# Adding x1 in the store's place: four y buffers, an accumulating DMA, and VectorE turning hid in the final stage of an expert-choice MoE layer

## The chip, the cores and the metric

The kernel runs on one core of a Trainium2 chip. The metric is the device time of one execution in microseconds. The core has TensorE (PE: matmuls and, in its own row, weight loads), VectorE (DVE), ScalarE (ACT), GpSimd (POOL) and SyncE (SP). SP and POOL issue the DMAs; the DMAs of both run on 16 DMA engines.

## What is computed

One encoder layer for two groups of 1024 tokens with 1024 columns, all in float32. A first part (token mixer) leaves `x1`, the residual stream, and `h2`, its normed and modulated form, in DRAM. The part that matters here is the last line of the layer:

```
x = x + gate2 * rmsnorm(expert_choice_moe(h), g_post_ffn)

def expert_choice_moe(h, w_router, w_gate, w_up, w_down):
    aff = jax.nn.softmax((xf @ w_router), axis=-1)
    gate, idx = lax.top_k(aff.T, cap)              # 16 experts, 128 rows each per group
    xe = xf[idx]
    hid = silu(xe @ w_gate) * (xe @ w_up)          # per expert
    ye = (hid @ w_down) * gate[..., None]
    y = zeros.at[idx].add(ye)                      # scatter-add into y
```

Each group picks its own 128 rows for every expert. A row of `y` is final when the last expert that picked it has been added. The result row is `x1 + rows * y / sqrt(mean(y*y) + eps)`, where `rows` is gate2 times the gain.

## The kernel before, in words

The stage `experts` (names with `moe_`) goes through experts 0 to 15 in order, both groups at a time. Experts 0 to 7 run in a loop on every engine, 8 to 15 are written out. Every float32 product is made of three products of a high and a low part, so each 1024x1024 weight matrix (GATE, UP, DOWN) comes as four pieces of 1 MB (`wf`), is rounded by ACT (`w_hi`, function `split`) and subtracted by DVE (`w_lo`, function `split`). A piece takes 24 matmuls of PE (PIECE 2 x 3 products x 4 banks). The PE order per expert e is UP(e), GATE(e+1), DOWN(e): 288 matmuls of 128x512.

Before DOWN(e), `hid` (128 rows by 1024 columns for each group) must be turned so that its columns lie on partitions. There are two ways in the kernel:

- Experts 0 to 7: DVE turns it with 16 transposes (`turn_h`, line 2581) into `h_raw`, ACT copies `h_hi` from it (`h_out`, line 2423), DVE subtracts `h_lo` (line 2587). PE starts DOWN with `down_first`, which waits for `h_hi_ready`.
- Experts 8 to 15 (`is_late`, LATE = 8): PE turns it with 16 transposes of 128x128 against the identity (`turn_h`, line 2754) into the PSUM banks, between the second and third piece of GATE(e+1); ACT and DVE take it out of PSUM (`turned_out`, lines 2411 and 2559).

From expert 9 on, final rows are put out beside the experts' work: the "window" of expert e holds four units, the last two experts' windows end at unit 25. A unit is 128 rows: units 0 to 15 are plain blocks of 128 tokens (valid for what experts up to 8 have added), units 16 to 25 are the row lists of experts 9 to 14, written again over the earlier rows; units 26 and 27 (expert 15's rows) come after the last matmul. For each unit, in the kernel before:

- POOL loads y into `fy` and x1 into `fx` (`load_unit`, lines 2337 to 2342), two buffers each; unit n waits for the store of unit n-2.
- ACT squares and sums `fy` (`square`, line 2458), DVE makes the mean (`mean`, line 2602), POOL takes the power -0.5 (`root`, line 2352).
- DVE scales (line 2610) and adds x1 (line 2616), both in `result`; POOL stores (`store_unit`, lines 2359 and 2365). The stores of one group's row lists wait for each other, since a row may stand in two lists.

POOL runs everything in written order: it waits for the scatter-add of expert e-1, loads two units, gathers half of expert e+2's rows, takes two roots, stores two units, the same again for the other two, and then issues the two scatter-adds of expert e (`scatter`, line 2325). ACT has its squares between pieces of weights, DVE its means and results. In the body of expert 15, POOL loads the last two units of the window (24 and 25), then y and x1 of units 26 and 27 (`load_last`), and only then takes roots and stores.

## Time and profile before

| what | value |
|---|---|
| device time, median of 3 runs | 2362.34 us (2360.07 to 2362.45) |
| device time of the profiled execution | 2362.63 us |
| its span, first to last instruction | 2360.9 us |
| PE busy | 2255.7 us (96%) |
| DVE busy | 1349.1 us (57%) |
| ACT busy | 1100.5 us (47%) |
| POOL busy | 730.6 us (31%) |
| mean granted TensorE clock | 0.988 of full speed |

The span is what the trace covers; the device time is 1.73 us more. Busy time is the sum of an engine's instructions; in the timeline a row's bracket is the idle time before it and who ended it. DMA-issuing instructions of POOL appear with the time that making their descriptors took. "To landing" is the time from a DMA's issue to its completion.

### The profile page before, as it was taken

The page shows a single profiled execution, that of the slowest core. Times are in us where ns is not written, and L with a number is a line of the kernel's source. Part 1 is how long each engine was busy: PE and PEld are TensorE (multiplying, and loading weights), DVE is VectorE, ACT ScalarE, POOL GpSimd, SP SyncE. Part 2 cuts the span into 40 slices and gives each one's busy share as a digit, 9 for nine tenths or more (in the row PEclk, how much of TensorE's full clock was granted, in tenths as well). Part 3 has the DMA queues.
Part 4 walks back from the last instruction along what each step waited for, and adds up shares of the span by engine and source line. Part 5 has one row for each costly group of instructions (what it writes and reads, how often), then busy time and mean ns, then how long its engine had stood idle before and what let it go on. Part 6 is the DMA issues. An engine that isn't in the chain of part 4 may idle for free. (4 is left out here: it accounts for less than half of the span.)

```text
span 2360.9 us, 34620 instructions
## 1 busy us (share of the span) xinstructions
PE 2255.7 (96%) x13219; PEld 1876.9 (79%) x13219; DVE 1349.1 (57%) x1995; ACT 1100.5 (47%) x1782; POOL 730.6 (31%) x770
## 2 busy tenths in 40 slices
PE   6999999999999999999984999999999999999997
PEld 4679989867899898677763888888888888888885
DVE  3212344555422436665557877777777667677665
ACT  4212434555534436665542544544444455545552
POOL 3004241434233515340003222221222333443634
PEclk9999999999999999999996999999999999999998
DMA  8745445657554459764538666766667678988785
GB/s 314 265 114 184 153 148 192 188 137 185 139 188 152 148 172 247 225 183 162 169 128 313 215 218 231 248 223 224 209 224 244 229 267 316 334 311 302 286 304 178
DMA packets 224095, 511.49 MB, mean 217 GB/s; under 512 B 38420, under 2 KB 129444, under 8 KB 204496
## 3 DMA queue, kind: packets, MB, share of 16 engines
q1 hardware_dynamic: 174576, 394.78, 49.3%
q0 software_dynamic: 49376, 114.78, 16.5%
q8 instruction: 92, 1.51, 0.3%
q14 instruction: 51, 0.42, 0.1%
HBM read 415.32 MB, written 93.69 MB: 216 GB/s over the span
## 5 line engine op out<-in xcount | busy, mean ns | idle before, releaser
L2553 DVE TENSOR_TENSOR moe_w_lo<-moe_wf,moe_w_hi 128x2048 fp32r<-128x2048 f32 x192 | 437.2, 2288 | 252.4 <-ACT moe_w_hi L2404 251.5
L2404 ACT ACTIVATE moe_w_hi<-moe_wf 128x2048 fp32r<-128x2048 f32 x192 | 366.0, 1915 | 436.7 <-PE moe_acc L2734 424.1
L2734 PE MATMUL moe_acc<-moe_w_hi,moe_x_hi 128*128 128x512 f32 x1024 | 400.1, 391 | 2.9 <-DVE moe_w_lo L2553 2.0
L2734 PE MATMUL moe_acc<-moe_w_lo,moe_x_hi 128*128 128x512 f32 x1024 | 399.2, 390 | 0.0
L2734 PE MATMUL moe_acc<-moe_w_hi,moe_x_lo 128*128 128x512 f32 x1024 | 399.1, 390 | 0.0
L2734 PEld LDWEIGHTS moe_acc<-moe_w_hi,moe_x_hi 128*128 128x128 f32 x1024 | 192.6, 188 | 43.7 <-DVE moe_w_lo L2553 2.4
L2734 PEld LDWEIGHTS moe_acc<-moe_w_hi,moe_x_lo 128*128 128x128 f32 x1024 | 192.6, 188 | 40.1
L2734 PEld LDWEIGHTS moe_acc<-moe_w_lo,moe_x_hi 128*128 128x128 f32 x1024 | 192.5, 188 | 39.7
L1793 PE MATMUL banks<-fr_w_hi,fr_h_hi 128*128 128x256 f32 x768 | 223.2, 291 | 0.0
L1793 PE MATMUL banks<-fr_w_lo,fr_h_hi 128*128 128x256 f32 x768 | 217.0, 283 | 0.0
L1793 PE MATMUL banks<-fr_w_hi,fr_h_lo 128*128 128x256 f32 x768 | 216.9, 282 | 0.0
L2308 POOL DMA_INDIRECT moe_xe<-scratch_h,moe_parts x120 | 181.5, 1513 | 86.8 <-issue 77.3
L1784 PE MATMUL banks<-fr_h_hi,fr_w_hi 128*128 128x512 f32 x496 | 204.3, 412 | 1.9 <-DVE fr_h_lo L1381 1.1
L1784 PE MATMUL banks<-fr_h_hi,fr_w_lo 128*128 128x512 f32 x496 | 194.2, 392 | 0.0
L1784 PE MATMUL banks<-fr_h_lo,fr_w_hi 128*128 128x512 f32 x496 | 193.7, 391 | 0.0
L1030 ACT ACTIVATE fr_stage<-banks 128x512 f32<-128x512 f32 (+1 forms) x114 | 67.4, 591 | 270.9 <-PE banks L1784 145.8
L1362 DVE TENSOR_TENSOR fr_w_lo<-fr_w_raw,fr_w_hi 128x1024 fp32r<-128x1024 f32 x56 | 71.2, 1274 | 209.3 <-ACT fr_w_hi L1018 209.3
L906 POOL DMA_DIRECT2D fr_v<-scratch_vov x224 | 156.2, 746 | 81.9 <-PE banks L1963 80.5
L2734 PE MATMUL moe_acc<-moe_w_hi,moe_h_hi 128*128 128x512 f32 x448 | 174.4, 389 | 0.0
L2734 PE MATMUL moe_acc<-moe_w_hi,moe_h_lo 128*128 128x512 f32 x448 | 174.3, 389 | 0.0
L2734 PE MATMUL moe_acc<-moe_w_lo,moe_h_hi 128*128 128x512 f32 x448 | 174.3, 389 | 0.0
L1793 PEld LDWEIGHTS banks<-fr_w_hi,fr_h_hi 128*128 128x128 f32 x768 | 146.8, 191 | 4.9 <-issue 4.8
(312 smaller groups left out, 4306.7 us busy)
## 6 DMA issues: line engine op xcount, KB each, us to landing
moe_wf<-in_w_expert_gate SPq DMA_DIRECT2D x64, 1024.0 KB, 5.3
moe_wf<-in_w_expert_up SPq DMA_DIRECT2D x64, 1024.0 KB, 6.0
moe_wf<-in_w_expert_down SPq DMA_DIRECT2D x64, 1024.0 KB, 6.8
fr_w_raw<-in_w_units SPq DMA_DIRECT2D x28, 1024.0 KB, 6.7
fr_bias<-in_na_bias SPq DMA_DIRECT2D x16, 1520.0 KB, 11.7
fr_a_w<-in_w_ada POOLq DMA_DIRECT2D x16, 1024.0 KB, 8.4
scratch_qk_t<-fr_stage SPq DMA_DIRECT2D x64, 256.0 KB, 2.5
scratch_vov<-fr_stage SPq DMA_DIRECT2D x96, 128.0 KB, 2.4
```

The source lines that it names most:

```text
L906: pool.dma_start(v[j][p0:CHUNK, CH_AT[rb] + n, :], v_view[2, m, r0:r0 + k, cols_, :]).then_inc(nv_loaded[j], 16)
L1030: nc.scalar.activation(out, product, ACT.Copy).then_inc(evac_done, 1)
L1362: nc.vector.tensor_tensor(w_lo[:, h % 2, k, :], w_raw[:, h % 2, k, :], w_hi[:, h % 2, k, :].bitcast(F32), ALU.subtract).then_inc(w_lo_read ...
L1784: mm = nc.tensor.matmul(ps[:, b % 2, :], w[x1][:, slot, k, a * P:(a + 1) * P], h[x2][:, k, t * HALF:(t + 1) * HALF], start=start, stop=stop)
L1793: mm = nc.tensor.matmul(ps[:, b % 2, part * QW:(part + 1) * QW], h[x1][:, k, tile:tile + P], w[x2][:, slot, k, :], start=(k == 0 and i == ...
L2308: pool.indirect_dma_start(quarter_rows(g)[:, t, :], None, h2_quarters, bass.IndirectOffsetOnAxis(ap=at, axis=0)).then_inc(gathered[g], 16)
L2404: nc.scalar.activation(w_hi[:, q, :, :], wf[:, q, :, :], ACT.Copy).then_inc(w_hi_ready, 1)
L2553: nc.vector.tensor_tensor(w_lo[:, q, :, :], wf[:, q, :, :], w_hi[:, q, :, :].bitcast(F32), ALU.subtract).then_inc(w_lo_ready, 1)
L2734: mm = nc.tensor.matmul(acc[:, j, b, :], x[:, g, k, :], w[:, q, a, h * HALF:(h + 1) * HALF], start=(k == 0 and i == 0), stop=(k == KC - 1 ...
```

## The change

It does four things.

- `fx` is gone and `fy` has four buffers (SLOTS = 4). `load_unit` loads y alone; unit n waits for the store of unit n-4. A window's four loads are issued together, then the whole gather, four roots, four `add_x1`, four stores.
- x1 is added to the scaled `fy` in SBUF by a DMA that accumulates (`add_x1`, new), issued by POOL when DVE has scaled the unit; the store waits for that DMA. DVE's add (line 2616) stays only for unit 26.
- The mean of units 0 to 25 is made by POOL in `root` (a multiply-add before the power) and no longer by DVE.
- `hid` of experts 8 to 14 is turned by DVE as it is for 0 to 7; only expert 15's is still turned by PE. ACT's squares move behind DOWN pieces 1 and 2, DVE's scalings behind DOWN pieces 2 and 3.

```
-    LATE = 8
+    SLOTS = 4
...
-        fy = s.sb("fy", [P, 2, D])
-        fx = s.sb("fx", [P, 2, D])
+        fy = s.sb("fy", [P, SLOTS, D])
...
-            return (fy[:, n % 2, :], fx[:, n % 2, :]) if n < LAST else (xe[:, n - LAST, :], ye[:, n - LAST, :])
+            return (fy[:, n % SLOTS, :], fy[:, n % SLOTS, :]) if n < LAST else (xe[:, n - LAST, :], ye[:, n - LAST, :])
...
             def load_unit(n):
-                j = n % 2
                 g, t, e = units[n]
-                if n >= 2:
-                    pool.wait_ge(out_stored[j], 16 * (n // 2))
+                if n >= SLOTS:
+                    pool.wait_ge(*used(out_stored, n - SLOTS))
+                loaded = used(fy_loaded, n)[0]
                 if t is not None:
-                    pool.dma_start(fy[:, j, :], y_view[t]).then_inc(fy_loaded[j], 16)
-                    pool.dma_start(fx[:, j, :], x1_view[t]).then_inc(fx_loaded[j], 16)
+                    pool.dma_start(fy[:, n % SLOTS, :], y_view[t]).then_inc(loaded, 16)
                 else:
                     at = bass.IndirectOffsetOnAxis(ap=index_c[:, col(e, g)], axis=0)
-                    pool.indirect_dma_start(fy[:, j, :], None, io["y"], at).then_inc(fy_loaded[j], 16)
-                    pool.indirect_dma_start(fx[:, j, :], None, io["x1"], at).then_inc(fx_loaded[j], 16)
+                    pool.indirect_dma_start(fy[:, n % SLOTS, :], None, io["y"], at).then_inc(loaded, 16)
+
+            def add_x1(n):
+                g, t, e = units[n]
+                pool.wait_ge(y_scaled, n + 1)
+                added_x1 = used(x1_added, n)[0]
+                if t is not None:
+                    pool.dma_start(fy[:, n % SLOTS, :], x1_view[t], accum_op=ALU.add).then_inc(added_x1, 16)
+                else:
+                    at = bass.IndirectOffsetOnAxis(ap=index_c[:, col(e, g)], axis=0)
+                    pool.indirect_dma_start(fy[:, n % SLOTS, :], None, io["x1"], at, compute_op=ALU.add).then_inc(added_x1, 16)
 
...
             def root(n):
-                pool.wait_ge(y_mean, n + 1)
-                nc.gpsimd.tensor_tensor(y_r[:, n % 2:n % 2 + 1], y_ss[:, n % 2:n % 2 + 1], mhalf[:, :], ALU.pow).then_inc(y_root, 1)
+                mean = y_ss[:, n % SLOTS:n % SLOTS + 1]
+                if n < LAST:
+                    pool.wait_ge(y_sq, n + 1)
+                    nc.gpsimd.tensor_scalar(mean, mean, 1.0 / D, EPS, ALU.mult, ALU.add)
+                    pool.drain()
+                else:
+                    pool.wait_ge(y_mean, n - LAST + 1)
+                nc.gpsimd.tensor_tensor(y_r[:, n % SLOTS:n % SLOTS + 1], mean, mhalf[:, :], ALU.pow).then_inc(y_root, 1)
 
             def store_unit(n):
-                j = n % 2
                 g, t, e = units[n]
-                pool.wait_ge(out_ready, n + 1)
+                stored = used(out_stored, n)[0]
+                if n < LAST:
+                    pool.wait_ge(*used(x1_added, n))
+                else:
+                    pool.wait_ge(out_ready, n - LAST + 1)
                 if t is not None:
-                    pool.dma_start(out_view[t], result_of(n)[1]).then_inc(out_stored[j], 16)
+                    pool.dma_start(out_view[t], result_of(n)[1]).then_inc(stored, 16)
                 else:
-                    pool.wait_ge(out_stored[j], 16 * (n // 2))
-                    if units[n - 1][0] == g:
-                        pool.wait_ge(out_stored[1 - j], 16 * ((n + 1) // 2))
+                    for m in range(n - SLOTS, n):
+                        if units[m][0] == g or m == n - SLOTS:
+                            pool.wait_ge(*used(out_stored, m))
                     at = bass.IndirectOffsetOnAxis(ap=index_c[:, col(e, g)], axis=0)
-                    pool.indirect_dma_start(io["out"], at, result_of(n)[1], None).then_inc(out_stored[j], 16)
+                    pool.indirect_dma_start(io["out"], at, result_of(n)[1], None).then_inc(stored, 16)
...
-                    for h, half in enumerate((ns[0:2], ns[2:4])):
-                        for n in half:
-                            load_unit(n)
-                        if not is_last(e, 2):
-                            gather(e + 2, j, range(h, h + 1))
-                        if is_last(e) and half:
-                            pool.wait_ge(x_turned, ONE + e * GROUPS)
-                            for g in range(GROUPS):
-                                load_last(g)
-                        for n in half:
-                            root(n)
-                        for n in half:
-                            store_unit(n)
+                    for n in ns:
+                        load_unit(n)
+                    if not is_last(e, 2):
+                        gather(e + 2, j)
+                    if is_last(e):
+                        pool.wait_ge(x_turned, ONE + e * GROUPS)
+                        for g in range(GROUPS):
+                            load_last(g)
+                    for n in ns:
+                        root(n)
+                    for n in ns:
+                        add_x1(n)
+                    for n in ns:
+                        store_unit(n)
...
                     split(e, DOWN, range(0, 1))
-                    if not is_late(e):
-                        h_out(e)
+                    h_out(e)
+                    split(e, DOWN, range(1, 2))
                     for n in ns[0:2]:
                         square(n)
-                    split(e, DOWN, range(1, 2))
-                    if is_late(e):
-                        turned_out(e - LATE, (h_hi, j), late_h_turned, late_h_hi_ready)
-                    split(e, DOWN, range(2, NP))
-
-                    silu(e + 1, 1 - j)
-                    split(e + 1, UP, range(0, 2))
+                    split(e, DOWN, range(2, 3))
                     for n in ns[2:4]:
                         square(n)
-                    split(e + 1, UP, range(2, NP))
+                    split(e, DOWN, range(3, NP))
+
+                    silu(e + 1, 1 - j)
+                    split(e + 1, UP)
...
+                j = n % SLOTS
                 dve.wait_ge(y_sq, n + 1)
-                nc.vector.tensor_scalar(y_ss[:, n % 2:n % 2 + 1], y_ss[:, n % 2:n % 2 + 1], 1.0 / D, EPS, ALU.mult, ALU.add).then_inc(y_mean, 1)
-
-            def result(n):
-                j = n % 2
+                nc.vector.tensor_scalar(y_ss[:, j:j + 1], y_ss[:, j:j + 1], 1.0 / D, EPS, ALU.mult, ALU.add).then_inc(y_mean, 1)
+
+            def scale(n):
+                j = n % SLOTS
                 dve.wait_ge(y_root, n + 1)
                 if n == 0:
                     dve.wait_ge(rows_loaded, 16 * GROUPS)
-                y_rows, x_rows = result_of(n)
-                nc.vector.scalar_tensor_tensor(y_rows, y_rows, y_r[:, j:j + 1], rows[:, units[n][0], :], ALU.mult, ALU.mult)
-                dve.drain()
+                y_rows = result_of(n)[0]
+                return nc.vector.scalar_tensor_tensor(y_rows, y_rows, y_r[:, j:j + 1], rows[:, units[n][0], :], ALU.mult, ALU.mult)
+
+            def result(n):
                 if n < LAST:
-                    dve.wait_ge(fx_loaded[j], 16 * (n // 2 + 1))
+                    scale(n).then_inc(y_scaled, 1)
                 else:
+                    scale(n)
+                    dve.drain()
                     dve.wait_ge(last_loaded[1][n - LAST], 16)
-                nc.vector.tensor_tensor(x_rows, x_rows, y_rows, ALU.add).then_inc(out_ready, 1)
+                    y_rows, x_rows = result_of(n)
+                    nc.vector.tensor_tensor(x_rows, x_rows, y_rows, ALU.add).then_inc(out_ready, 1)
...
-                    if is_late(e):
-                        split(e + 1, GATE, range(2, NP))
-                        multiply(e, j)
-                    else:
-                        split(e + 1, GATE, range(2, 3))
-                        multiply(e, j)
-                        split(e + 1, GATE, range(3, NP))
-                        turn_h(e)
+                    split(e + 1, GATE, range(2, 3))
+                    multiply(e, j)
+                    split(e + 1, GATE, range(3, NP))
+                    turn_h(e)
                     split(e, DOWN, range(0, 1))
-                    if not is_late(e):
-                        h_out(e)
-                    for n in ns[0:2]:
-                        mean(n)
-                    split(e, DOWN, range(1, 2))
-                    if is_late(e):
-                        turned_out(e - LATE, h_hi, h_lo, j, late_h_hi_ready, late_h_ready)
+                    h_out(e)
+                    split(e, DOWN, range(1, 3))
                     for n in ns[0:2]:
                         result(n)
-                    split(e, DOWN, range(2, NP))
-                    split(e + 1, UP, range(0, 2))
-                    for n in ns[2:4]:
-                        mean(n)
+                    split(e, DOWN, range(3, NP))
                     for n in ns[2:4]:
                         result(n)
-                    split(e + 1, UP, range(2, NP))
+                    split(e + 1, UP)
...
-            weighted, j = fy[:, 0, :], (LAST + 1) % 2
+            j = (LAST + 1) % SLOTS
+            weighted = fy[:, j, :]
+            dve.wait_ge(*used(out_stored, LAST + 1 - SLOTS))
...
-                    products(e + 1, GATE, 1 - j, x_hi[:, 1 - j], x_lo[:, 1 - j], first)
-                    if is_late(e):
-                        turn_h(e, j)
-                    products(e + 1, GATE, 1 - j, x_hi[:, 1 - j], x_lo[:, 1 - j], second)
-                    if is_late(e):
-                        pe.wait_ge(late_h_ready, ONE + (e - LATE) * BK + BK)
-                        products(e, DOWN, j, h_hi, h_lo)
-                    else:
-                        down_first(e, j)
-                        products(e, DOWN, j, h_hi, h_lo, range(1, NP))
+                    products(e + 1, GATE, 1 - j, x_hi[:, 1 - j], x_lo[:, 1 - j])
+                    down_first(e, j)
+                    products(e, DOWN, j, h_hi, h_lo, range(1, NP))```

What stands in VectorE's row in the window of expert 13, from the product with UP on, before (`moe_w_lo` is a piece of weights, `moe_hid` the product silu times up, `moe_h_lo` the low part of the turned hid):

```order
L2598 TENSOR_TENSOR moe_hid<-moe_hid,moe_acc 128x512 x4
L2553 TENSOR_TENSOR moe_w_lo<-moe_wf,moe_w_hi 128x2048
L2602 TENSOR_SCALAR moe_parts<-moe_parts 128x1 x2
L2553 TENSOR_TENSOR moe_w_lo<-moe_wf,moe_w_hi 128x2048
L2559 TENSOR_TENSOR moe_h_lo<-moe_acc,moe_h_hi 128x512 x4
L2610 SCALAR_TENSOR_TENSOR moe_fy<-moe_fy,moe_parts,moe_rows 128x1024
L2616 TENSOR_TENSOR moe_fx<-moe_fx,moe_fy 128x1024
L2610 SCALAR_TENSOR_TENSOR moe_fy<-moe_fy,moe_parts,moe_rows 128x1024
L2616 TENSOR_TENSOR moe_fx<-moe_fx,moe_fy 128x1024
L2553 TENSOR_TENSOR moe_w_lo<-moe_wf,moe_w_hi 128x2048 x4
```

And at the same place in the changed kernel (line 2566 is the piece of weights, 2594 the transposes, 2600 the low part, 2624 the scaling):

```order
L2611 TENSOR_TENSOR moe_hid<-moe_hid,moe_acc 128x512 x4
L2566 TENSOR_TENSOR moe_w_lo<-moe_wf,moe_w_hi 128x2048
L2594 STREAM_TRANSPOSE moe_h_raw<-moe_hid 32x16x32 x16
L2566 TENSOR_TENSOR moe_w_lo<-moe_wf,moe_w_hi 128x2048
L2600 TENSOR_TENSOR moe_h_lo<-moe_h_raw,moe_h_hi 128x1024 x2
L2566 TENSOR_TENSOR moe_w_lo<-moe_wf,moe_w_hi 128x2048 x2
L2624 SCALAR_TENSOR_TENSOR moe_fy<-moe_fy,moe_parts,moe_rows 128x1024 x2
L2566 TENSOR_TENSOR moe_w_lo<-moe_wf,moe_w_hi 128x2048
L2624 SCALAR_TENSOR_TENSOR moe_fy<-moe_fy,moe_parts,moe_rows 128x1024 x2
L2566 TENSOR_TENSOR moe_w_lo<-moe_wf,moe_w_hi 128x2048 x4
```

Sixteen transposes came in ahead of DOWN's first piece, the means and the adds of x1 are gone, the first two scalings stand one piece of DOWN later, and the other two now come before UP's pieces.

What POOL issues at the program's end before, from the loads of units 24 and 25 on (`moe_xe` and `moe_ye` here are y and x1 of units 26 and 27):

```order
L2341 DMA moe_fy<-scratch_y,moe_parts 128x1024
L2342 DMA moe_fx<-scratch_x,moe_parts 128x1024
L2341 DMA moe_fy<-scratch_y,moe_parts 128x1024
L2342 DMA moe_fx<-scratch_x,moe_parts 128x1024
L2347 DMA moe_xe<-scratch_y,moe_parts 128x1024
L2348 DMA moe_ye<-scratch_x,moe_parts 128x1024
L2347 DMA moe_xe<-scratch_y,moe_parts 128x1024
L2348 DMA moe_ye<-scratch_x,moe_parts 128x1024
L2352 TENSOR_TENSOR moe_parts<-moe_parts 128x1 x2
L2365 DMA out<-moe_fx,moe_parts 2048x1024 x2
L2352 TENSOR_TENSOR moe_parts<-moe_parts 128x1
L2365 DMA out<-moe_ye,moe_parts 2048x1024
```

In the changed kernel (lines 2340 y, 2355 and 2356 the last units, 2362 the mean, 2366 the root, 2350 the accumulating add of x1, 2382 the store):

```order
L2340 DMA moe_fy<-scratch_y,moe_parts 128x1024 x2
L2355 DMA moe_xe<-scratch_y,moe_parts 128x1024
L2356 DMA moe_ye<-scratch_x,moe_parts 128x1024
L2355 DMA moe_xe<-scratch_y,moe_parts 128x1024
L2356 DMA moe_ye<-scratch_x,moe_parts 128x1024
L2362 TENSOR_SCALAR moe_parts<-moe_parts 128x1
L2366 TENSOR_TENSOR moe_parts<-moe_parts 128x1
L2362 TENSOR_SCALAR moe_parts<-moe_parts 128x1
L2366 TENSOR_TENSOR moe_parts<-moe_parts 128x1
L2350 DMA moe_fy<-scratch_x,moe_parts 128x1024 x2
L2382 DMA out<-moe_fy,moe_parts 2048x1024 x2
L2366 TENSOR_TENSOR moe_parts<-moe_parts 128x1
```

Two loads of x1 left the row ahead of the roots, and two adds by DMA stand between the roots and the stores of units 24 and 25.

## Rows read from the trace of the kernel before

**Rows 1.** The page: PE's busy time, share of the span, instructions.

```profile
PE 2255.7 (96%) x13219; PEld 1876.9 (79%) x13219; DVE 1349.1 (57%) x1995; ACT 1100.5 (47%) x1782; POOL 730.6 (31%) x770
```

**Rows 2.** The chain that ended last, windows of experts 9 on: start, us, what.

```profile
1928.40 1.75 PE moe_acc L2754 x16
1930.15 65.30 PE moe_acc L2734 x288
```

**Rows 3.** Stretches: PE, PEld, DVE, ACT, POOL busy, PEclk, DMA share, GB/s.

```profile
1333.00:1858.00 525.00, 525.00 (x2317) 434.69 (x2317) 395.36 (x305) 248.58 (x193) 135.50 (x106) 1.00 0.68 228
1992.00:2059.00 67.00, 67.00 (x306) 55.68 (x305) 48.60 (x36) 35.65 (x35) 25.32 (x26) 1.00 0.88 315
```

**Rows 4.** Timeline, DVE, ACT and PE, expert 6: start, us, engine, line.

```profile
1719.94 2.48 DVE L2598 TENSOR_TENSOR moe_hid<-moe_hid,moe_acc 128x512 f32<-128x512 f32 x4 [1.14 <-PE moe_acc L2734]
1724.71 11.45 DVE L2581 STREAM_TRANSPOSE moe_h_raw<-moe_hid 32x512 f32<-32x512 f32 x16
1736.19 2.29 DVE L2553 TENSOR_TENSOR moe_w_lo<-moe_wf,moe_w_hi 128x2048 fp32r<-128x2048 f32 x1
...
1736.20 2.01 ACT L2423 ACTIVATE moe_h_hi<-moe_h_raw 128x1024 fp32r<-128x1024 f32 x2 [8.90 <-DVE moe_h_raw L2581]
...
1741.50 0.39 PE L2766 MATMUL moe_acc<-moe_w_hi,moe_h_hi 128*128 128x512 f32 x1
```

**Rows 5.** Groups by line, forms apart: xcount | busy us, mean ns | idle before.

```profile
L2616 DVE TENSOR_TENSOR moe_fx<-moe_fx,moe_fy 128x1024 f32<-128x1024 f32 x26 | 31.9, 1226 | 2.3 <-issue 0.4
L2352 POOL TENSOR_TENSOR moe_parts<-moe_parts 128x1 f32<-128x1 f32 x28 | 17.5, 632 | 55.2 <-DVE moe_parts L2602 54.1 <-DVE moe_parts L2697 1.0
```

**Rows 6.** Timeline, POOL, ACT and PE, end of expert 14's window.

```profile
2288.34 0.94 POOL L2341 DMA_INDIRECT moe_fy<-scratch_y,moe_parts  x1 [1.34 <-DMA out<-moe_fx,moe_parts]
...
2296.98 1.06 ACT L2458 ACTIVATE moe_zero<-moe_fy 128x1024 f32<-128x1024 f32 x1 [4.13 <-DMA moe_fy<-scratch_y,moe_parts]
...
2305.56 0.61 PE L2734 MATMUL moe_acc<-moe_w_hi,moe_x_hi 128*128 128x512 f32 x1 [1.98 <-DVE moe_w_lo L2553]
...
2308.95 0.52 PE L2734 MATMUL moe_acc<-moe_w_hi,moe_x_lo 128*128 128x512 f32 x1
...
2346.99 0.39 PE L2734 MATMUL moe_acc<-moe_w_hi,moe_h_lo 128*128 128x512 f32 x1
```

**Rows 7.** Timeline, POOL, the program's last 60 us.

```profile
2301.10 1.81 POOL L2365 DMA_INDIRECT out<-moe_fx,moe_parts  x1 [1.18 <-DVE moe_fx L2616]
2306.47 2.07 POOL L2365 DMA_INDIRECT out<-moe_fx,moe_parts  x1 [3.56 <-DMA out<-moe_fx,moe_parts]
2308.85 1.60 POOL L2325 DMA_INDIRECT scratch_y<-moe_ye,moe_parts  x1 [0.30 <-issue]
...
2321.17 2.40 POOL L2341 DMA_INDIRECT moe_fy<-scratch_y,moe_parts  x1 [8.83 <-DMA scratch_y<-moe_ye,moe_parts]
...
2334.97 1.11 POOL L2352 TENSOR_TENSOR moe_parts<-moe_parts 128x1 f32<-128x1 f32 x2
...
2340.96 0.97 POOL L2365 DMA_INDIRECT out<-moe_fx,moe_parts  x1 [0.67 <-DVE moe_fx L2616]
2343.73 0.57 POOL L2352 TENSOR_TENSOR moe_parts<-moe_parts 128x1 f32<-128x1 f32 x1 [1.80 <-DVE moe_parts L2602]
...
2351.50 1.01 POOL L2365 DMA_INDIRECT out<-moe_ye,moe_parts  x1 [1.67 <-DVE moe_ye L2703]
```

**Rows 8.** DMA by queue, 1767 to 1779 us (an expert's two scatter-adds beside weights).

```profile
q0 software_dynamic: 288, 1.05, 49.7%
q1 hardware_dynamic: 277, 1.59, 37.6%
...
scratch_y<-moe_ye,moe_parts POOLq DMA_INDIRECT x2, 6.5
```

**Rows 9.** DMA issues, 2193 to 2303 us: xcount, median us to landing.

```profile
out<-moe_fx,moe_parts POOLq DMA_INDIRECT x7, 4.5
...
moe_fx<-scratch_x,moe_parts POOLq DMA_INDIRECT x6, 10.1
```

45 lines of the change are left out of this document (21 added, 24 removed).

## The prediction

> **What bounds the kernel now.** I read the page first: PE is busy 2255.7 of 2360.9 us [rows 1]. In the stretch that the change touches the chain that ended last is PE without a gap: 65.30 us of 288 matmuls for each expert, and between them 1.75 us of 16 transposes of `hid` [rows 2]. So an expert from 8 on takes 67.05 us, one of those before 65.3, and one matmul steps by 65.30/288 = 0.227 us. The stretches say the same: PE fills both, DVE is busy 395.36 of 525 us where it turns `hid` itself and 48.60 of 67 where PE does [rows 3]. DMA is the engine to watch beside them: its share is 0.68 in the early stretch and 0.88 in a window with units [rows 3].
>
> There are two places where PE doesn't set the time. The first is in expert 14's window: the load of unit 23 waits for a store [rows 6], its square on ACT starts at 2296.98 after waiting 4.13 us for the data, ACT's next weights are late, and PE idles 1.98 us before 2305.56. Behind that come nine matmuls, up to the one at 2308.95, which step by (2308.95-2305.56)/8 = 0.42 us and not 0.227: TensorE ran at its lower level, and lost 9*0.2 = 1.8 us more. The second is the end. PE's last matmul ends at 2346.99+0.39 = 2347.4, and POOL was by then on a chain of its own: store of unit 23 waiting for a store (2306.47), scatter-add of expert 14 (2308.85), its landing (2321.17), eight loads, roots (2334.97), store 25 (2340.96), root of unit 26 (2343.73), last store (2351.50) [rows 7]. From that last store to the end of the span are 9.4 us, which no part of the change touches.
>
> **The change, part by part.** *Turning on DVE.* PE loses 7*16 transposes, 7*1.75 = 12.25 us, all on the chain. DVE gets 16 transposes at 11.45 us per expert, and `h_lo` from SBUF. Whether PE then waits is read from expert 6, where the same order runs [rows 4]. UP ends at about U = 1719.9, where DVE begins to multiply; the transposes end at U+16.3; the weights of DOWN's first piece are ready at 1736.19+2.29 = U+18.6, `h_hi` at 1736.20+2.01 = U+18.3; PE starts DOWN at 1741.50 = U+21.6. So there are 3.0 us of slack, and nothing in a window stands ahead of this point on DVE or ACT: squares and scalings come behind DOWN's second piece. Behind it I walk the row. DVE: `h_lo` 2.35 to U+20.9, two pieces 4.6 to U+25.5, but ACT's piece comes after two squares (1.06 and a read of 0.2 each), so U+26.9; PE wants that piece at U+32.7. Two scalings at 1.28 and a piece: U+31.8, wanted at U+38.1. Slack is 5 to 6 us throughout. VectorE's busy time is 48.6+11.45-4*1.23 [rows 5] = 55 of 65.3 us. I cost this part at 12.25 us gained.
>
> *Four buffers.* Loads of a window no longer wait for stores of the same window. The squares of units 22 and 23 come from loads issued at the window's start, so the stall before UP(15) and its slow matmuls go: 1.98+1.8 = 3.8 us. PE would then end at 2347.4-12.25-3.8 = 2331.3.
>
> *x1 by an accumulating DMA.* DVE's 26 adds (31.9 us) were hidden behind PE and are worth nothing there. In their place stand 26 DMAs that read x1 and `fy` and write `fy`. The trace has no such DMA into SBUF; the nearest row is the scatter-add, 0.5 MB each. In the 12 us with two of them, queue q0 took 49.7% for 1.05 MB, that is 5.96 us of all 16 engines or 3.0 us apiece, while q1 moved 1.59 MB of weights in 37.6%, 2.8 us per MB, 1.4 us for 0.5 MB [rows 8]. Time to landing: 6.5 us for the scatter-adds when little else runs [rows 8], 10.1 for loads of x1 in the window [rows 9]. From below an add costs what the load that it replaces cost (nothing more), from above 12 us to landing, the wait from the issue of the last scatter-add to 2321.17. I take 10 us in a window and 6.5 to 7 at the end, where the weights are all in.
>
> *Means on POOL.* One more small operation of at most the root's 0.63 us [rows 5] for each unit, and one less hand-over from DVE to POOL; at the end 1.2 us for units 24 and 25 in a row, elsewhere hidden by POOL's own waits.
>
> **The end, worked out.** U is the end of UP(14). Before, UP(15) began two half pieces (5.4 us) before the idle time, at 2298.1, so U = 2298.1-43.5-1.75 = 2252.85, and the scatter-add of 14 at 2308.85 was at U+56. After, U comes six turns earlier: 2242.35. Scalings end at U+28.2, 29.5, 33.1, 34.4; their adds land near U+39 to U+46. Units 20, 22 and 23 belong to one group, so their stores go one after the other, 4.5 us each [rows 9] with 10.8 as the worst that I take: two landings, then the issue of the third (2306.47 to 2308.85 is 2.4). That gives U+52 with quick stores and U+57 with 7 us each; I take U+55, 2297.4, or 11.5 us earlier than before.
>
> From the scatter-add to the roots before were 2334.97-2308.85 = 26.1 us with eight loads, at about 1.7 us each from 2321.17. Two fall away: 22.7, and with the means 24. Root of 25 at 2321.4. Then, in place of "scale, add, scale, add" on DVE: two scalings 2.6, issue of the adds, 6.5 to 7 us to landing, two store issues and the 2.8 us that POOL took from its store (2340.96) to the root of unit 26 (2343.73). This is about 13.2 us in place of 8.8. Root of 26 at about 2334.5, against 2343.73: 9.2 us earlier. Unit 26's mean is ready long before (PE's bank for it at 2326), so POOL's chain and not PE sets the end, and all behind that root is as before. Span 2360.9-9.2 = 2351.7; the profiled execution's time lies 1.7 us above its span: **2353.4 us**. Its own 2362.63 is 0.3 above the median 2362.34, so this is 9 us or 0.4% below. Of the 16.05 us that PE gives back, 7 are lost behind POOL.
>
> The row against the rule: an indirect DMA of 0.5 MB took 6.5 us to landing with little beside it [rows 8]. The Trainium skill, "DMA: Bandwidth & Descriptors", section "Anatomy of one DMA — SWDGE (gpsimd) path", fits 2.0 us plus bytes over 436 GB/s, which makes 3.2 us for 0.5 MB. By that page the two adds at the end would land 3.3 us sooner and the time would be 2350, an estimate. The trace doesn't bear the page out for this kind of DMA.
>
> **Rivals.** *PE sets the end after all.* If adds and stores are quick, the scatter-add of 14 goes as soon as `ye` is ready, near U+48, and POOL's root of 26 is at 2327.5, when its mean is there. Then the end is PE's: 2331.3+13.5 (2347.4 to 2360.9) = 2344.8, time 2346.5. For it speaks that the loads of units 24 and 25 took about 5 us in the quiet end; against it that three stores of one group and the adds in front of them can hardly all fit into 48-28 us. 13 in 100.
>
> *The adds are slow and eat the gain.* In expert 15's body ACT takes the squares of 24 and 25 before it takes the turned `hid` out of PSUM. By my walk unit 25 is in at 2317.5 and squared at 2318.5, and PE needs the low part at 2331.3-10.9 = 2320.4, with 1.9 us of work between: no slack. If the scatter-add of 14 comes 5 us later than I take it, both chains move by that, PE stalls and TensorE falls to its lower level again (1.8 us). Then 2358 to 2361. Stores that took 9 to 11 us in a busy window would do it. 15 in 100.
>
> *DMA becomes the bound: slower.* A window's DMA share of 0.88 is 59 us of work [rows 3]. Four adds in place of four loads bring 4*(3.0-1.4) = 6.4 us more: 65.4 in a period of 65.3. Each further us of DMA work is then a us of PE waiting for weights, with slow matmuls behind each stall. It decides when an add costs over 3.4 us of the 16 engines: at 4.5 us a window takes 71.4, which is 4.3 us more than 67.05, over five windows 22 us, less the 12 gained elsewhere: 2371. For it speaks the sum; against it that when busy the engines move more than the mean suggests, and that weights have slack: ACT waited for PE, not for data, before its pieces. 10 in 100. The rule that bears on it is in the Trainium skill, same page, section "Issuing engines are not separate DMA queues": transfers issued from several engines share the 16 DMA engines and interleave. By that rule, the trace agrees: the two queues' shares add up to 87% there.
>
> **How the numbers follow.** The forecast (gain of 6 to 12.5 us) gets 62 in 100, PE at the end 13, the slow adds 15, DMA as the bound 10. What a measurement of this kernel can tell from no change is about 0.2%, 4.7 us. Slow adds fall on both sides of it, mostly inside. So: faster 0.78, same 0.13, slower 0.09. The range runs from PE's bound, 2346, to the slow adds' end, 2361, and leaves out most of the DMA case.
>
> **What would show it.** Right: no matmul of line 2754's kind before expert 15; 65.3 us per expert in the chain; no idle time of PE before UP(15); the end's chain through POOL's add of x1 and its landing. Each step by itself: the scatter-add of 14 near 2297, the root of 26 near 2334, adds landing in 10 and 7 us. Wrong: idle time of PE that ended on `w_lo` or `h_hi` in windows 9 to 13, granted clock below 1 there, a DMA share near 1, or ACT's turned copy in expert 15 behind a late square.

## The result and the profile after

The changed kernel takes 2394.27 us, the median of 4 runs (2392.56 to 2396.8), against 2362.39 for the kernel before in 4 runs beside it: a ratio of 1.0138 with an interval of 1.0126 to 1.0150. It is 32 us slower, where 9 us faster was forecast. The profiled execution has a span of 2390.9 us, 30.0 more than before's 2360.9.

The page of the changed kernel, busy time of each engine, to be held against [rows 1]:

```profile
PE 2252.6 (94%) x13107; PEld 1871.0 (78%) x13107; DVE 1393.4 (58%) x2041; ACT 1098.3 (46%) x1768; POOL 768.6 (32%) x796
```

The 112 transposes of PE are gone, as the change says, and still PE is busy for almost as long. The stretches of the changed kernel from expert 9's window on say why (columns as in [rows 3]):

```profile
1858.00:2391.00 533.00, 485.61 (x2099) 399.25 (x2097) 379.93 (x302) 246.32 (x228) 229.29 (x192) 0.95 0.80 266
...
2130.00:2200.00 70.00, 64.87 (x278) 53.19 (x278) 51.59 (x40) 35.33 (x32) 33.56 (x30) 0.95 0.85 291
...
2285.00:2354.00 69.00, 58.85 (x255) 48.01 (x253) 32.57 (x21) 28.54 (x28) 33.73 (x25) 0.94 0.74 224
```

PE idles in the windows of experts 11 to 14, and the granted clock is 0.95 and 0.94 in the two stretches shown, where [rows 3] had 1.00: part of the matmuls behind each stall run at TensorE's lower level. The waits of the changed kernel, 1850 to 2391 us (who waited for whom: us in total, times, longest):

```profile
POOL out L2376 <- DMA moe_fy<-scratch_x: 61.6, 16, 5.6
...
DVE moe_fy L2624 <- POOL moe_parts L2366: 52.6, 26, 10.9
...
ACT moe_w_hi L2422 <- DMA moe_wf<-in_w_expert_gate: 36.4, 13, 4.3
POOL moe_parts L2366 <- issue: 32.0, 9, 7.3
...
PE moe_acc L2740 <- DVE moe_w_lo L2566: 18.2, 4, 5.4
```

Read from the bottom: PE waited 18.2 us in four windows (11 to 14) for the low part of a piece of weights. DVE was late with it because its scalings stand ahead of it and waited 52.6 us for POOL's roots. POOL's roots waited 32.0 us for nothing that the profile shows. And the stores waited 61.6 us for the added x1.

**One window.** POOL in the window of expert 12 of the changed kernel, from its last gather on:

```profile
2148.43 0.96 POOL L2308 DMA_INDIRECT moe_xe<-scratch_h,moe_parts  x1 [0.30 <-issue]
2149.47 0.18 POOL L2362 TENSOR_SCALAR moe_parts<-moe_parts 128x1 f32<-128x1 f32 x1
2154.97 0.57 POOL L2366 TENSOR_TENSOR moe_parts<-moe_parts 128x1 f32<-128x1 f32 x1 [5.31 <-issue]
...
2163.55 3.65 POOL L2347 DMA_DIRECT2D moe_fy<-scratch_x  x4
2169.60 0.57 POOL L2376 DMA_DIRECT2D out<-moe_fy  x1 [2.40 <-DMA moe_fy<-scratch_x]
2173.66 0.55 POOL L2376 DMA_DIRECT2D out<-moe_fy  x1 [3.48 <-DMA moe_fy<-scratch_x]
2178.68 0.53 POOL L2376 DMA_DIRECT2D out<-moe_fy  x1 [4.47 <-DMA moe_fy<-scratch_x]
2183.68 0.53 POOL L2376 DMA_DIRECT2D out<-moe_fy  x1 [4.47 <-DMA moe_fy<-scratch_x]
2184.52 2.89 POOL L2325 DMA_INDIRECT scratch_y<-moe_ye,moe_parts  x1 [0.31 <-issue]
```

Between the mean (0.18 us) and the root of the first unit stands `pool.drain()`, and there 5.31 us pass. What the 16 DMA engines moved meanwhile, in the changed kernel from 2137 to 2160, in slices of 0.575 us:

```profile
GB/s 385 378 356 420 385 477 413 435 413 399 371 413 385 399 385 399 328 378 378 313 370 356 292 221 107 64 36 21 14 0 0 0 0 0 0 0 0 0 0 0
```

The last gather was issued by 2149.39; nothing is moved from the 30th slice on, 2153.7; the root starts 1.3 us later, at 2154.97. The same holds at two other long ones: nothing from about 2296.3 on and the root at 2297.32 (7.28 us behind the mean), nothing from 2363.2 on and the root at 2364.46 (6.07 behind). The weights' loads had stopped by then as well, but in the third case POOL's own loads were all that ran, and in the window of expert 10 it is the other way round: POOL's queue q0 had moved its last packets by 2010.6, the root started at 2011.56 (2.96 us of idle time), and the weights' queue q1 was 91% busy from 2010.6 to 2011.5. The drain let POOL go on only when its own DMAs were done. In the next units of a window, with nothing outstanding, it is not to be seen: mean 1.29 us, root 0.55, some 2.1 for both. What DVE and then PE do with that, in the same window:

```profile
2155.57 1.29 DVE L2624 SCALAR_TENSOR_TENSOR moe_fy<-moe_fy,moe_parts,moe_rows 128x1024 f32<-128x1024 f32 x1 [10.79 <-POOL moe_parts L2366]
...
2158.85 2.28 DVE L2566 TENSOR_TENSOR moe_w_lo<-moe_wf,moe_w_hi 128x2048 fp32r<-128x2048 f32 x1
...
2161.18 0.79 PE L2740 MATMUL moe_acc<-moe_w_hi,moe_h_hi 128*128 128x512 f32 x1 [5.13 <-DVE moe_w_lo L2566]
```

DVE stood still for 10.79 us in front of a scaling, DOWN's last piece came behind it at 2161.13, and PE had idled 5.13 us. The matmul behind the wait takes 0.79 us, not 0.39.

**POOL's round.** The chain of the changed kernel no longer runs through PE in the windows but round and round through POOL. From the scatter-add of expert 11 at 2112.30 to that of 12 at 2184.52 are 72.2 us: 19.8 until it has landed and the loads of y may go (2132.09), 17.3 for four loads and eight gathers (to 2149.4), 14.1 for means, drain and roots (to 2163.55), 21.0 for the adds, their landings one after the other and the stores. Each of these waits for the one before, and PE needs only 65.3. The scatter-adds go out at 1972.96, 2043.09, 2112.30, 2184.52: one per 69 to 72 us, and none waits for expert results any more. In the trace before, those of experts 9 to 12 all did:

```profile
2100.87 1.90 POOL L2325 DMA_INDIRECT scratch_y<-moe_ye,moe_parts  x1 [3.42 <-ACT moe_ye L2446]
```

So the round had 3.4 to 3.8 us of slack in these windows of 67.05 us, and windows of 65.3 would have left about 2, an estimate. The change put four waits for added x1 and about 12 us at the roots (14.1 in place of 4*0.63) into it.

**The window of expert 13.** It is longer still. From the scatter-add of 12 at 2184.52 to that of 13 at 2269.52 are 85.0 us. Before, these were 69.9 us (2167.96 to 2237.86), and the scatter-adds of 13 and 14 had no slack even then (0.30 us of "issue" in front of each, as in [rows 7]). The units of this window are row lists. Their four adds take POOL 9.5 us to issue, where the plain blocks' took 3.65, and stores of one group wait for each other, with nothing else of POOL's between them now:

```profile
2265.70 0.95 POOL L2382 DMA_INDIRECT out<-moe_fy,moe_parts  x1 [11.96 <-DMA out<-moe_fy,moe_parts]
```

Before, the loads and roots of the window's second half stood between the two pairs of stores, and no store waited for another store there. Against before, the scatter-adds of experts 9 to 14 are late by 6.2, 9.3, 11.4, 16.6, 31.7 and 31.9 us: half of what reaches the end arises in this one window. It is as long in kernels below that undo another part: 78.3 us with the means on VectorE, 83.1 with x1 by a plain DMA, 84.9 with PE turning. How much of it is the row of four stores alone, no run shows.

**The adds.** DMA issues and queues of the changed kernel, 2163 to 2190 (the last number of an issue is the median time to landing):

```profile
q0 software_dynamic: 902, 3.31, 53.2%
q1 hardware_dynamic: 783, 5.42, 49.0%
...
moe_fy<-scratch_x POOLq DMA_DIRECT2D x4, 512.0 KB, 11.4
out<-moe_fy POOLq DMA_DIRECT2D x4, 512.0 KB, 13.3
```

In the stretch the two queues' shares add up to 102%, against 87% in [rows 8]. The Trainium skill says in "DMA: Bandwidth & Descriptors", section "Issuing engines are not separate DMA queues", that DMAs of different issuing engines run on the same 16 DMA engines and interleave. By that rule, the trace agrees. Over all 16 direct adds the median is 12.4 us to landing, with 13.2 for the stores behind them. ACT waits for GATE's weights there, the 36.4 us above; it is not what PE waited for.

**The end.** POOL, ACT, DVE and PE of the changed kernel, timeline, from the last stores of expert 14's window:

```profile
2333.82 1.12 POOL L2382 DMA_INDIRECT out<-moe_fy,moe_parts  x1 [9.97 <-DMA out<-moe_fy,moe_parts]
2339.24 1.23 POOL L2382 DMA_INDIRECT out<-moe_fy,moe_parts  x1 [4.30 <-DMA out<-moe_fy,moe_parts]
2340.78 2.55 POOL L2325 DMA_INDIRECT scratch_y<-moe_ye,moe_parts  x1 [0.30 <-issue]
...
2350.87 1.01 POOL L2340 DMA_INDIRECT moe_fy<-scratch_y,moe_parts  x1 [5.66 <-DMA scratch_y<-moe_ye,moe_parts]
...
2355.22 1.06 ACT L2474 ACTIVATE moe_zero<-moe_fy 128x1024 f32<-128x1024 f32 x1 [16.08 <-DMA moe_fy<-scratch_y,moe_parts]
...
2358.97 1.06 ACT L2429 ACTIVATE moe_h_hi<-moe_acc 128x512 fp32r<-128x512 f32 x2
2359.59 1.29 DVE L2572 TENSOR_TENSOR moe_h_lo<-moe_acc,moe_h_hi 128x512 fp32r<-128x512 f32 x2 [17.74 <-ACT moe_h_hi L2429]
...
2360.93 0.79 PE L2740 MATMUL moe_acc<-moe_w_hi,moe_h_hi 128*128 128x512 f32 x1 [13.04 <-DVE moe_h_lo L2572]
...
2374.45 0.39 PE L2740 MATMUL moe_acc<-moe_w_hi,moe_h_lo 128*128 128x512 f32 x1
```

The scatter-add of 14 is out at 2340.78, forecast 2297. The y of unit 24 stands behind it, ACT's square of unit 24 behind that, the turned `hid` of expert 15 behind the square, and PE idles 13.04 us.

**The sum.** PE's last matmul ends at 2374.84, 27.5 us later than before's 2347.38. What follows it takes 16.1 us in place of 13.5. Together 30.0. The stretch has 2099 matmuls of PE, and so has the same stretch of a kernel below in which none of them waits (the one with scatter-adds first):

```profile
1858.00:2400.00 542.00, 473.79 (x2099) 392.13 (x2097) 381.25 (x328) 246.80 (x228) 204.82 (x166) 0.98 0.79 262
```

There PE's last matmul ends at 2331.8. The 43.0 us between that and 2374.8 are 18.2+13.0 of idle time and 485.61-473.79 = 11.8 us for which matmuls took longer, the slow ones behind the waits.

### The profile page after: what moved, and what is told of

Its sections match the earlier page's. It is cut to its first block and busy times, and to the rows that moved or that the text cites. A ratio compares the mean times of both kernels' runs of the same rounds, so it can differ in the third digit from the quotient of the medians.

```text
span 2390.9 us, 34466 instructions
## 1 busy us (share of the span) xinstructions
PE 2252.6 (94%) x13107; PEld 1871.0 (78%) x13107; DVE 1393.4 (58%) x2041; ACT 1098.3 (46%) x1768; POOL 768.6 (32%) x796
## 5 line engine op out<-in xcount | busy, mean ns | idle before, releaser
L2422 ACT ACTIVATE moe_w_hi<-moe_wf 128x2048 fp32r<-128x2048 f32 x192 | 365.6, 1915 | 391.9 <-PE moe_acc L2740 330.7
L2566 DVE TENSOR_TENSOR moe_w_lo<-moe_wf,moe_w_hi 128x2048 fp32r<-128x2048 f32 x192 | 435.9, 2288 | 184.3 <-ACT moe_w_hi L2422 183.2
L2740 PE MATMUL moe_acc<-moe_w_hi,moe_x_hi 128*128 128x512 f32 x1024 | 398.7, 389 | 0.9 <-DVE moe_x_lo L2572 0.6
L2740 PE MATMUL moe_acc<-moe_w_lo,moe_x_hi 128*128 128x512 f32 x1024 | 398.4, 389 | 0.0
L2740 PE MATMUL moe_acc<-moe_w_hi,moe_x_lo 128*128 128x512 f32 x1024 | 398.4, 389 | 0.0
L2740 PEld LDWEIGHTS moe_acc<-moe_w_hi,moe_x_hi 128*128 128x128 f32 x1024 | 192.2, 188 | 41.2 <-DVE moe_x_lo L2572 0.8
L2740 PEld LDWEIGHTS moe_acc<-moe_w_hi,moe_x_lo 128*128 128x128 f32 x1024 | 192.2, 188 | 40.0
L2740 PEld LDWEIGHTS moe_acc<-moe_w_lo,moe_x_hi 128*128 128x128 f32 x1024 | 192.2, 188 | 39.9
L2308 POOL DMA_INDIRECT moe_xe<-scratch_h,moe_parts x120 | 175.9, 1466 | 86.9 <-issue 77.2
L2740 PE MATMUL moe_acc<-moe_w_hi,moe_h_hi 128*128 128x512 f32 x392 | 157.8, 403 | 31.2 <-DVE moe_w_lo L2566 18.2
L2594 DVE STREAM_TRANSPOSE moe_h_raw<-moe_hid 32x512 f32<-32x512 f32 x240 | 168.7, 703 | 4.5
L2740 PE MATMUL moe_acc<-moe_w_lo,moe_h_hi 128*128 128x512 f32 x392 | 156.3, 399 | 0.0
L2740 PE MATMUL moe_acc<-moe_w_hi,moe_h_lo 128*128 128x512 f32 x392 | 156.3, 399 | 0.0
```

The costliest lines, as they stand in the source:

```text
L2308: pool.indirect_dma_start(quarter_rows(g)[:, t, :], None, h2_quarters, bass.IndirectOffsetOnAxis(ap=at, axis=0)).then_inc(gathered[g], 16)
L2422: nc.scalar.activation(w_hi[:, q, :, :], wf[:, q, :, :], ACT.Copy).then_inc(w_hi_ready, 1)
L2566: nc.vector.tensor_tensor(w_lo[:, q, :, :], wf[:, q, :, :], w_hi[:, q, :, :].bitcast(F32), ALU.subtract).then_inc(w_lo_ready, 1)
L2594: a = nc.vector.transpose(h_raw[u * QT:(u + 1) * QT, :, :, t * QT:(t + 1) * QT], columns)
L2740: mm = nc.tensor.matmul(acc[:, j, b, :], x[:, g, k, :], w[:, q, a, h * HALF:(h + 1) * HALF], start=(k == 0 and i == 0), stop=(k == KC - 1 ...
```

## The experiments

**Which part costs it.** Four kernels undo one part each, or do one part alone. First, the changed kernel with the means of units 0 to 25 on VectorE as before:

```
             def root(n):
-                if n < LAST:
-                    pool.wait_ge(y_sq, n + 1)
-                    nc.gpsimd.tensor_scalar(mean, mean, 1.0 / D, EPS, ALU.mult, ALU.add)
-                    pool.drain()
-                else:
-                    pool.wait_ge(y_mean, n - LAST + 1)
+                pool.wait_ge(y_mean, n + 1)
...
-                    split(e, DOWN, range(1, 3))
+                    split(e, DOWN, range(1, 2))
+                    for n in ns[0:2]:
+                        mean(n)
+                    split(e, DOWN, range(2, 3))
```

> The changed kernel with one part undone: the mean of units 0 to 25 is made by VectorE again (behind DOWN's pieces 1 and 2), and GpSimd's root is one power, with no drain. Theory A (GpSimd's drain between mean and power waits for the gathers that it has just issued, 5.3 us at 2149.65, and the roots behind it are late for VectorE's scaling): PE's idle time before DOWN's last piece (5.1 us a window) goes, windows last 65.3 to 67, the time falls from 2394 to 2355 to 2372. Theory B (the accumulating DMAs alone make GpSimd's round of 71 us): the windows stay at 70 us or more and the time at 2388 to 2396.

Measured: 2369.41 us, ratio 1.0030 (1.0016 to 1.0044), 24.9 us below the changed kernel. Its waits of PE:

```profile
PE moe_acc L2742 <- DVE moe_h_lo L2567: 12.6, 1, 12.6
...
PE moe_acc L2742 <- DVE moe_w_lo L2561: 3.2, 1, 3.2
```

The stalls of the windows are down from 18.2 to 3.2 us (one, in window 14); the one in expert 15 stays. So the means on POOL carry most of the loss as the changed kernel stands, and without them it is still 0.3% slower than before.

Second, x1 brought by a plain DMA. It overwrites the scaled y, so the normed part is missing in the rows of units 0 to 25; sizes and places of all transfers stay.

```
-  pool.dma_start(fy[:, n % SLOTS, :], x1_view[t], accum_op=ALU.add).then_inc(added_x1, 16)
+  pool.dma_start(fy[:, n % SLOTS, :], x1_view[t]).then_inc(added_x1, 16)
...
-  pool.indirect_dma_start(fy[:, n % SLOTS, :], None, io["x1"], at, compute_op=ALU.add).then_inc(added_x1, 16)
+  pool.indirect_dma_start(fy[:, n % SLOTS, :], None, io["x1"], at).then_inc(added_x1, 16)
```

> The changed kernel with x1's DMA as a plain copy into fy in the place of the accumulating one: same bytes from DRAM, same waits, same order; the scaled y is overwritten, so the normed part of rows 0 to 25's units is left out of the result. Theory B: copies land in about half the time of the adds (13.7 us before), GpSimd's round gets shorter by 10 us or more, scatter-adds go out when ye is ready, windows are PE's 65.3 us, time 2345 to 2360. Theory A alone: the drain is still there, PE's stalls stay, time 2385 to 2394.

Measured: 2357.76 us, ratio 0.9988 (0.9978 to 0.9998), 36.5 below the changed kernel. The direct transfers land in 7.0 us, not 12.4, the scatter-adds of experts 9 to 12 go out every 65.3 us (1962.61, 2027.85, 2093.13, 2158.41), and PE's waits on `w_lo` are 0.5 us in all although the drain is still there. The wait in expert 15 stays with 11.0 us: the scatter-add of 14 goes at 2310.35, behind the long window 13. Either this repair or the first alone almost closes the stalls of the windows: they don't add up as prices; they are two loads on one round, for which there are 65.3 us. This undoing gives back more than the first, so neither part alone is "the" loss.

Third, the kernel before with the one line `LATE = NE - 1`, so that VectorE turns `hid` for experts 8 to 14 and nothing else changes (two buffers, x1 loaded, means on VectorE).

> The kernel before with LATE = 15 in place of 8: hid of experts 8 to 14 is turned by VectorE, everything else stays (two buffers each, x1 added and means made by VectorE). If the first part of my sum is right (12.25 us of transposes off PE, 3.0 us of slack): 65.3 us a window, PE's last matmul 12 us earlier, time 2348 to 2357. If VectorE's row is too full with its own adds and means in it: PE idle before DOWN's pieces in each window, time 2362 or more.

Measured: 2381.31 us, ratio 1.0085 (1.0068 to 1.0102): 19 us slower than before. Its waits, 1850 to 2400 us:

```profile
DVE moe_parts L2602 <- ACT moe_zero L2458: 57.5, 11, 8.4
ACT moe_zero L2458 <- DMA moe_fy<-scratch_y: 43.5, 8, 7.4
...
PE moe_acc L2734 <- DVE moe_w_lo L2553: 19.1, 7, 9.5
...
PE moe_acc L2734 <- DVE moe_x_lo L2573: 6.4, 4, 1.8
```

With two buffers the round goes through VectorE: results come 12 us later behind the transposes, so the stores, the next loads, ACT's squares and the means do too, and DVE waits at a mean with weights queued behind it. PE pays 25.5 us of waits for 12.25 us of transposes.

Fourth, the changed kernel with PE turning `hid` for 8 to 14 as before (`is_late` and LATE = 8 back, all else as changed).

> The changed kernel with the turning undone: hid of experts 8 to 14 is turned by PE again, the rest (four y buffers, accumulating DMA, means on GpSimd) as changed. Theories A and B both say that GpSimd's round of 71 to 72 us sets the windows, so PE's extra 1.75 us go into its idle time: 2390 to 2400. Rival C (VectorE's 11.5 us of transposes are what makes its row late): the stalls go, time 2360 to 2375.

Measured: 2377.35 us, ratio 1.0073 (1.0056 to 1.0090), 16.9 below the changed kernel and well below what I had expected. PE has no wait in the windows, one of 12.4 us in expert 15, and the scatter-adds of experts 9 to 12 wait 1.1 to 2.9 us for results again: a window of 67.05 us is just enough for POOL's round there, one of 65.3 is not. VectorE doesn't wait for a root from 1930 to 2200, where it waited 32.2 us in the changed kernel. What keeps this kernel above before comes behind that: its scatter-add of 12 is 1.4 us earlier than before's, its window 13 takes 84.9 us, and the scatter-add of 14 is 15.2 us late. The run by itself would also fit VectorE's transposes as the cause of the stalls; against that stand the kernels below in which VectorE turns and PE waits nowhere.

**The drain.** The changed kernel, mean still on POOL, with a semaphore in the drain's place:

```
-                    nc.gpsimd.tensor_scalar(mean, mean, 1.0 / D, EPS, ALU.mult, ALU.add)
-                    pool.drain()
+                    nc.gpsimd.tensor_scalar(mean, mean, 1.0 / D, EPS, ALU.mult, ALU.add).then_inc(y_mean, 1)
+                    pool.wait_ge(y_mean, n + 1)
```

> The changed kernel with GpSimd's drain between mean and power replaced by a semaphore that the mean sets and the power waits for; the mean stays on GpSimd. If the drain is what costs (it lasts until the gathers issued before it have landed: 5.3, 7.3 and 6.1 us in three windows), most of e1's gain comes: 2368 to 2376. If it is the second small operation on GpSimd that costs (1.1 us each, some 2.4 beside VectorE's work), the time stays above 2385.

Measured: 2374.07 us, ratio 1.0042 (1.0026 to 1.0059), 20.2 below the changed kernel. POOL in this kernel, the same place as above:

```profile
2140.96 0.18 POOL L2362 TENSOR_SCALAR moe_parts<-moe_parts 128x1 f32<-128x1 f32 x1
2141.23 0.57 POOL L2366 TENSOR_TENSOR moe_parts<-moe_parts 128x1 f32<-128x1 f32 x1
```

The 5.31 us are 0.09. So 20.2 of the 24.9 us that the means cost (22.7 of 25.5 by the ratios, each against its own runs of before) are the drain's wait for POOL's DMAs. The 3 to 5 us that are left for the work itself, 2.0 us a unit here with its root, are not clear of the noise.

**The order of the queues.** Three kernels build on the first (means on VectorE). In expert 15's body ACT takes the turned `hid` out before the squares of units 24 and 25:

```
                     split(e, DOWN, range(2, NP))
+                    turned_out(0, (h_hi, j), last_h_turned, last_h_hi_ready, range(2, BK))
                     for n in ns:
                         square(n)
-                    turned_out(0, (h_hi, j), last_h_turned, last_h_hi_ready, range(2, BK))
```

> e1_mean_dve with one more change: in expert 15 ScalarE takes the turned hid out of PSUM before it squares units 24 and 25 (in e1 it sat 16.9 us in the square of 24 at 2331.44 and PE then 12.6 us). Theory: that order alone makes PE's last stall, so PE's idle time there goes and its last matmul comes near 2335 in place of 2350.4. But the end is on GpSimd's chain (scatter-add of 14 at 2317, y of 24 at 2327, root of 26 at 2350), which only gains the 3 us by which VectorE scaled unit 24 late: time 2363 to 2368. If PE's stall sets the end by itself, the time falls by 12 us or more, to 2357 or less.

Measured: 2367.66 us, ratio 1.0019 (1.0008 to 1.0031). PE's stall in expert 15 is gone and its last matmul starts at 2337.59, 12.5 us sooner than in the first kernel, and yet the time falls by 1.7 us only (2.6 by the ratios), which the intervals can't tell from nothing. POOL's chain holds the end: scatter-add of 14 at 2316.79, root of unit 26 at 2349.01. PE's 13 us in expert 15 were a side effect of that late scatter-add and cost little beside it. One stall is left, 5.2 us in window 14.

Then, on top, POOL issues the scatter-adds of expert e ahead of the window's stores:

```
+                if not is_last(e):
+                    scatter(e, j)
                 for n in ns:
                     store_unit(n)
-                if not is_last(e):
-                    scatter(e, j)
```

> e5_act_order with GpSimd's scatter-adds of expert e ahead of the stores of its window and not behind them. Theory: what makes the chain late is that the scatter-add waits in GpSimd's row for x1's adds and for the stores of one group, 9 to 11 us each. Then the scatter-add of 14 is issued near 2295 in place of 2317, the loads of 24 and 25 come when the stores are through, near 2317 in place of 2327, and the time is 8 to 12 us less than e5: 2353 to 2359. If DMA bandwidth is what makes them late, the stores slip by what the scatter-add gains and the time stays within 3 us of e5.

Measured: 2355.41 us, ratio 0.9971 (0.9958 to 0.9983): 12 us below the kernel before it and 7 below before. Timeline of POOL and PE in this kernel:

```profile
2094.56 1.89 POOL L2325 DMA_INDIRECT scratch_y<-moe_ye,moe_parts  x1 [11.53 <-ACT moe_ye L2457]
...
2290.39 1.86 POOL L2325 DMA_INDIRECT scratch_y<-moe_ye,moe_parts  x1 [3.63 <-ACT moe_ye L2457]
...
2331.40 0.39 PE L2742 MATMUL moe_acc<-moe_w_hi,moe_h_lo 128*128 128x512 f32 x1
```

The scatter-adds wait for results again, with 11.5 us of slack in the windows of experts 9 to 12 and 3.6 in the last two, in place of none. All windows take 65.28 us, that of expert 13 too, and PE waits nowhere. The adds' landings and the stores are still in the queue, but no longer between an expert's result and the next window's loads.

Third, on top of that, units 24 and 25 with x1 loaded into the two free buffers and added by VectorE.

> e6_scatter_first with units 24 and 25 as in the kernel before: x1 loaded into the two free buffers and added by VectorE, no accumulating DMA for them. In e1 their adds stood 7.5 us between scaling and store. Expected: root of 26 some 5 to 7 us earlier than in e6, time 2346 to 2354, below the kernel before (2361). If the loads of x1 take as long on GpSimd as the adds did, nothing is gained.

Measured: 2354.87 us, ratio 0.9965 (0.9953 to 0.9978), not to be told from the run before it, where I had expected the root of unit 26 5 to 7 us earlier. The two landings at the end are gone, but two loads more stand ahead of the roots, and VectorE's scaling and adding make unit 26's mean late: POOL waits 1.66 us for it and takes that root at 2333.93, against 2335.80.

**The two prices with nothing else in the way.** On the kernel with scatter-adds first, `hid` of 8 to 14 turned by PE again:

> This is the kernel of the run with scatter-adds first (mean on VectorE, squares of 24 and 25 behind the turned hid, scatter-adds ahead of the window's stores), with hid of experts 8 to 14 turned by TensorE again. It prices the turn by itself, where nothing else makes PE wait. If turning on VectorE is free there, as the prediction's term has it, PE gets 7*1.75 = 12.25 us more work, its last matmul ends near 2331.4+12.3 = 2343.7 and POOL's chain, which hangs on expert 14's results, moves along: 2366 to 2369. If VectorE's turning costs its own waits even here, the difference is smaller: 2357 to 2362.

Measured: 2365.24 us, ratio 1.0019 (1.0008 to 1.0029). From ratio to ratio that is 0.0048 or 11.3 us above the same kernel with VectorE turning. PE's last matmul:

```profile
2343.96 0.39 PE L2755 MATMUL moe_acc<-moe_w_hi,moe_h_lo 128*128 128x512 f32 x1
```

2343.96-2331.40 = 12.56, where 7*1.75 = 12.25 was the term. The scatter-adds of experts 9 to 11 wait 17.8 us for results here: 6.3 more than with VectorE turning, 1.8 of them the longer window.

And x1 by a plain DMA (the rows of units 0 to 25 lack their normed part, as above):

> The same kernel as the run with scatter-adds first, with x1 brought by a DMA that does not accumulate. It overwrites the scaled y, so the rows of units 0 to 25 lack their normed part; all transfers have the same sizes and places. If the accumulating kind costs time only at the end there, by two landings of 6.5 in place of about 4 us: 2351 to 2354. If it costs nothing where the scatter-adds no longer stand behind it: 2354.5 to 2356.5. If it still held the whole window back: 2346 to 2349, near the bound by PE's last matmul (2331.4+13.5+1.7 = 2346.6).

Measured: 2350.59 us, ratio 0.9958 (0.9944 to 0.9972), 3 us below by the ratios; the two intervals overlap, so the size is uncertain. Over one whole window of 65.3 us, first of the kernel with accumulating adds (queue: packets, MB, share of 16 engines; issue: KB each, us to landing):

```profile
q0 software_dynamic: 2379, 8.32, 44.7%
...
moe_fy<-scratch_x POOLq DMA_DIRECT2D x4, 512.0 KB, 12.3
```

and of the one with plain transfers:

```profile
q0 software_dynamic: 2400, 8.39, 37.6%
...
moe_fy<-scratch_x POOLq DMA_DIRECT2D x4, 512.0 KB, 7.3
```

The accumulating kind took (44.7-37.6)% of 65.3 us for four, 1.2 us more of the 16 engines each, and 5.0 us more to landing. Both kernels run their windows in 65.28 us, so a difference can only come from the two landings at the end: the roots of unit 26 are at 2335.80 and 2332.95. In the second trace PE's last matmul is 2.7 us later (2334.08 against 2331.40), so counted from there the root comes 5.5 us sooner.

Last, the kernel before with only its scatter-adds moved ahead of the window's last two stores.

> The kernel before with one edit: POOL issues the scatter-adds of a window's expert ahead of the last two stores and no longer behind them. If POOL's chain set the end before, as the prediction reads it, the scatter-add of 14 goes some 5 to 8 us sooner than 2308.85 and the time falls to 2354 to 2358. If PE's last matmul at 2347.4 holds the end there (the rest behind it was 13.5 us), it stays within 2 us: 2360 to 2363. If the stores then free the two buffers later and loads and squares come late, PE waits more in the windows: 2364 or above.

Measured: 2367.66 us (2363.16 to 2371.45 in 6 runs), ratio 1.0032 (1.0019 to 1.0045): slower than before. POOL's timeline of this kernel:

```profile
2303.57 3.34 POOL L2325 DMA_INDIRECT scratch_y<-moe_ye,moe_parts  x1 [3.76 <-ACT moe_ye L2448]
...
2320.78 2.66 POOL L2365 DMA_INDIRECT out<-moe_fx,moe_parts  x1 [10.45 <-DMA out<-moe_fx,moe_parts]
2323.75 0.97 POOL L2341 DMA_INDIRECT moe_fy<-scratch_y,moe_parts  x1 [0.31 <-issue]
```

The scatter-add of 14 is 5.3 us sooner than in [rows 7], but the last store waits 10.45 us for another behind it, and the loads of unit 24 come 2.6 us later. The edit pays where adds and stores hold up the scatter-add; before, only two stores did. The profiled execution was the fastest of the six; what makes the others up to 8 us longer isn't seen in its trace and stays open.

## Why the prediction was wrong

**Turning on DVE: right, under a condition that it did not state.** 16 transposes took 703 ns each as expected, `h_hi` and `h_lo` were never late in the windows, and the 12.25 us came out as 12.6 at PE and 11.3 in time once nothing else waited. Alone, with two buffers, it cost 19 us. The sentence "I cost this part at 12.25 us gained" held DVE's and ACT's rows against PE and left out POOL's: a PE that needs 65.3 us per expert asks the same of every round beside it.

**Four buffers: the term right, its price not seen.** No stall is left before UP(15), and with the other causes taken away PE's last matmul starts at 2331.4 and ends at 2331.8, where 2331.3 was worked out. But the buffers came with a new order, four stores in a row ahead of the scatter-adds. The prediction walked these only in window 14 ("4.5 us each") and left window 13 at 65.3 us; it took 85.0.

**Means on POOL: the step that failed.** It put POOL's added work in the windows at nothing. The prediction has "one more small operation of at most the root's 0.63 us" and "elsewhere hidden by POOL's own waits". The operation was 0.18 to 1.3 us, but the drain behind it held POOL for 2.1 to 7.3 us at the first unit of every window and at the end, 31.7 us in all, the roots now stood behind the whole gather, and DVE had its scalings ahead of DOWN's last piece. I walked DVE with scalings of 1.28 us that are always ready; the one shown waited 10.8. In the changed kernel this was worth 24.9 us, 20.2 of it the drain. The trace before had a row that showed the drain's kind of wait. In the loop over experts 0 to 7 a small copy on POOL is followed by a drain, right behind two scatter-adds:

```profile
1771.50 1.58 POOL L2325 DMA_INDIRECT scratch_y<-moe_ye,moe_parts  x1 [0.30 <-issue]
1772.52 1.53 POOL L2303 COPY moe_parts<-moe_parts 128x8 uint32 x1
1779.24 1.38 POOL L2308 DMA_INDIRECT moe_xe<-scratch_h,moe_parts  x1 [5.20 <-issue]
```

The 5.20 us of "issue" there are about what the scatter-adds of [rows 8] take to land.

**x1 by an accumulating DMA: the engines' share right, the landing too short, its place in the queue not seen.** I had 3.0-1.4 = 1.6 us more of 16 engines for each and measured 1.2, so the rival of DMA as the bound falls: windows of 65.28 us run with all the adds in them, at a DMA share of 0.95 to 0.96. But 10 us to landing were 12.4, with 13.2 for the direct stores behind them, whose median in the trace before was 3.0, and above all the scatter-adds stood behind four such landings. "I take U+55" for the scatter-add of 14 was 2297.4 and came out as 2340.8. Taking the accumulation away gives back 36.5 us while the drain is there, and about 3 after the repairs. The scatter-adds' 6.5 us, too, are not "with little beside": in the 12 us of [rows 8] the two queues fill 87% of the engines.

**The rivals.** "The adds are slow and eat the gain" had the mechanism of the end in full: ACT's squares of 24 and 25 ahead of the turned `hid`, PE idle, slow matmuls. It had the scatter-add 5 us late, and it was 43 late. It was also read as a cause; the fifth experiment shows PE's stall there to be worth about 2 us at most, since POOL's chain ends as late without it. At the end itself the two adds were quicker than I took: the first, its descriptors made by 2369.92, had landed by 2374.9, so in 5.0 us. The Trainium skill, "DMA: Bandwidth & Descriptors", section "Anatomy of one DMA — SWDGE (gpsimd) path", has a fit that gives 3.2 us for 0.5 MB, an estimate. The trace's 5.0 lies between it and my 6.5 to 7.

**What was missing in the method.** The forecast walked one engine's row per stage. The bound of a window here is a closed round: scatter-add, its landing, loads, gathers, roots, adds, their landings, stores, scatter-add. Its slack could be read in one row per window: 3.4 to 3.8 us for which the scatter-adds of experts 9 to 12 waited on results, and nothing at those of 13 and 14. The prediction used only the last of these rows, and as a fixed point. Every item put into that round counts in full beyond the slack, and each us beyond it comes back at PE with slow matmuls on top: 31.2 us of idle time brought 11.8 more.

## What to carry to other kernels

Before an instruction moves to another queue, follow that queue round once, from an expert to the next, and read from the trace what slack the round has; compare it with the period that the change itself promises. A drain on GpSimd cost here what its outstanding DMAs still needed, so a semaphore on the one instruction is the cheaper fence there. And where a transfer that others wait for stands behind stores that nobody waits for, change their order first: here that one edit was worth 12 us and turned a slower kernel into a faster one (2355.4 us, 0.29% below before). It isn't free everywhere: in the kernel before it cost 0.3%.

## What the runs showed of the hardware that I had not expected

- `drain` on GpSimd between two operations of 128x1 lasted 2.1 to 7.3 us in seven places where indirect DMAs issued by that engine were under way. In the four looked at closely it ended about 1 to 1.5 us after these had moved their last bytes, in one of them with the weights' DMAs still running. With a semaphore in its place the gap was 0.09 us.
- DMAs of 512 KB that accumulate from DRAM into SBUF landed in 12.3 us where plain ones took 7.3 in the same window; four issued within 3.65 us released their waiters 4.1 to 5.0 us apart. Of the 16 engines they took 1.2 us more each.
- Undoing the turn, the means or the accumulating adds gave back 16.9, 24.9 and 36.5 us: 78 us of a loss of 32, as each of them reopens the same round.
